# Where a decoder trunk computes the second layer's first eight modulation panels

## The reference

```python
mod = (silu(c) @ ada_w[l] + ada_b[l]).reshape(B, 9, D)      # 9 chunks of 1024: shift, scale, gate x 3
sh1, sc1, g1, sh2, sc2, g2, sh3, sc3, g3 = mod              # per sequence, broadcast over tokens
u = rmsnorm(x, ng[0]) * (1 + sc1) + sh1
x = x + 0.5 * g1 * swiglu(u, w_ffn_up[l, 0], w_ffn_down[l, 0])
u = rmsnorm(x, ng[1]) * (1 + sc2) + sh2
# in projection; conv, RWKV, pooling and attention branches; four gated branch products; out projection
merged = sum(sigmoid(u @ w_gate[l, i]) * (y_i @ w_branch[l, i]))
x = x + g2 * (merged @ w_out[l])
u = rmsnorm(x, ng[2]) * (1 + sc3) + sh3
x = x + 0.5 * g3 * swiglu(u, w_ffn_up[l, 1], w_ffn_down[l, 1])
```

## Time and profile before

| | |
|---|---|
| median of three runs | 3191.99 us |
| the profiled execution, its own time | 3193.19 us |
| its span (first to last instruction) | 3191.5 us |
| TensorE matmuls busy | 3124.6 us, 98% |
| VectorE, GpSimd, ScalarE busy | 1170.4, 858.4, 421.1 us |
| granted TensorE clock, mean | 0.993 |

### The profile page before, as it was taken

The page is one execution under the profiler, slowest core; times in us unless marked ns, Lnnn a source line. Parts: engine busy times, 40 slices in busy tenths (PEclk is TensorE's granted clock), DMA queues, the critical chain, the costliest instruction groups (busy, mean ns, idle before and its releaser), DMA issues.

```text
span 3191.5 us, 42629 instructions
## 1 busy us (share of the span) xinstructions
PE 3124.6 (98%) x17664; PEld 2478.5 (78%) x17664; DVE 1170.4 (37%) x2229; ACT 421.1 (13%) x806; POOL 858.4 (27%) x749
## 2 busy tenths in 40 slices
PE   7999999999999999999989999999999999999998
PEld 4777887677777878888867778876777778788887
DVE  3223422453233463343232233234533244633432
ACT  2000002302111120010010000023021111200100
POOL 2333430210000334444333334302100003344442
PEclk9999999999999999999999999999999999999999
DMA  6444322531111212222254442234311113122221
GB/s 268 182 161 185 112 86 93 172 124 39 51 51 58 103 66 80 80 90 75 87 225 160 170 178 106 86 107 146 126 53 51 37 60 111 67 79 81 88 73 65
DMA packets 72928, 337.43 MB, mean 106 GB/s; under 512 B 10528, under 2 KB 27680, under 8 KB 39584
## 3 DMA queue, kind: packets, MB, share of 16 engines
q1 hardware_dynamic: 63360, 312.03, 27.0%
q0 software_dynamic: 6816, 18.88, 2.0%
q10 hardware_dynamic: 2560, 3.80, 0.3%
HBM read 326.55 MB, written 6.02 MB: 104 GB/s over the span
## 4 chain that ended last, share of the span: by engine, by line
PE 96%; DVE 2%; DMA 1%; ACT 1%; issue 0%; SPq 0%; DVEq 0%
PE ps L670 95%; DVE ws L1683 1%; ACT ws L1404 0%; DMA ring<-w_ada 0%; DMA lp<-params 0%; DVE u L1683 0%; DVE proj L1683 0%; ACT u L1404 0%; PE ps L725 0%; DVE masked_room L2054 0%; DVE x L1686 0%; PE ps L1231 0%; DVE masked_room L1683 0%; DVE proj L1686 0%; DVE proj L1689 0%
## 5 line engine op out<-in xcount | busy, mean ns | idle before, releaser
L670 PE MATMUL ps<-u,ring 128*128 128x272 f32 x4608 | 1152.3, 400 | 23.4 <-ACT u L1404 17.4
L670 PEld LDWEIGHTS ps<-u,ring 128*128 128x128 f32 x4608 | 865.6, 192 | 238.8 <-issue 50.9
L1683 DVE TENSOR_TENSOR ws<-ws,ps 128x272 f32<-128x272 f32 (+2 forms) x778 | 347.3, 452 | 1484.6 <-PE ps L670 1477.9
L633 POOL TENSOR_TENSOR masked_room<-ring 128x512 f32<-128x512 f32 (+1 forms) x76 | 95.8, 1261 | 1312.2 <-DVE pause L2380 657.0
L670 PE MATMUL ps<-y,ring 128*128 128x272 f32 x1376 | 350.8, 393 | 0.0
L1404 ACT ACTIVATE ws<-ps 128x272 f32<-128x272 f32 (+1 forms) x398 | 154.9, 396 | 1322.0 <-PE ps L670 1321.7
L670 PE MATMUL ps<-y,masked_room 128*128 128x272 f32 x1296 | 315.8, 393 | 2.8 <-DVE ws L1683 2.8
L670 PE MATMUL ps<-y,ws 128*128 128x272 f32 x1296 | 315.6, 393 | 0.0
L670 PEld LDWEIGHTS ps<-y,ring 128*128 128x128 f32 x1376 | 261.3, 190 | 54.5 <-DVE proj L1683 0.7
L670 PEld LDWEIGHTS ps<-y,masked_room 128*128 128x128 f32 x1296 | 245.7, 190 | 55.4 <-issue 4.8
L670 PEld LDWEIGHTS ps<-y,ws 128*128 128x128 f32 x1296 | 245.9, 190 | 52.0 <-issue 1.6
(11 more groups left out here) (199 smaller groups left out, 2516.7 us busy)
## 6 DMA issues: line engine op xcount, KB each, us to landing
ring<-w_up SPq DMA_DIRECT2D x88, 1024.0 KB, 4.8
ring<-w_ada SPq DMA_DIRECT2D x72, 1024.0 KB, 4.8
ring<-w_down SPq DMA_DIRECT2D x32, 1024.0 KB, 4.7
ring<-w_gate SPq DMA_DIRECT2D x32, 1024.0 KB, 4.7
ring<-w_in SPq DMA_DIRECT2D x22, 1024.0 KB, 4.7
ws<-cache SPq DMA_DIRECT2D x128, 128.0 KB, 3.1
ws<-cache POOLq DMA_DIRECT2D x128, 128.0 KB, 3.4
ring<-w_down SPq DMA_DIRECT2D x16, 768.0 KB, 4.1
```

The costliest lines, as they stand in the source:

```text
L633: nc.gpsimd.tensor_tensor(sums[:, 0], a21, a22, ALU.add).then_inc(w_sums.sem, 1)
L670: return nc.tensor.matmul(out, lhsT, rhs, start=start, stop=stop, skip_group_check=skip)
L1683: return V.tensor_tensor(out, a, b, op)
```

## The change

Five edits:

1. The first 8 modulation panels of the second layer are computed in the first layer's up1, behind units 2, 4, ..., 16 (`NEXT_AT`), and their two chunks are turned and kept there. The second layer has no stage ada: it starts with `sum_squares`. The small part of `lp` (the layer's vectors) for it is loaded in up1. All numbers of loads and parts now run on over both layers.
2. `keep_clock` issues matmuls of constants (128 x 260) whose results nobody reads: 4 before each up0 and up1, 3 more inside unit 0 of the first up0, 3 before each in, 2 in the sample attention of each layer.
3. The gate of fill 5 goes into bank 6, and waits for the sigmoid of fill 3 only.
4. The final store of `x` is five DMAs: three of two tiles each, as they are done, then tile 7, then tile 6.
5. The large loads of constants and layer parameters stand before load 12 of up0, not before load 3.

```diff
+NEXT_AT = [[q // 2 - 1] if q in range(2, 18, 2) else [] for q in range(FT)]
+def panels_behind(l, f, q):
+    if f == 0:
+        return ADA_AT[q]
+    return NEXT_AT[q] if l + 1 < DEPTH else []
...
+        def gate_bank(f):
+            return 6 if f == 5 else 4
...
-                        if stage == "up0" and i == 3:
+                        if stage == "up1" and i == 3 and l + 1 < DEPTH:
+                            sp_.wait_ge(mix_done.sem, mix_done.upto(l, 1))
+                            sp_.dma_start(lp[:, 0:NVEC], lp_d[l + 1][:, 0:NVEC]).then_inc(lp_loaded.sem, 16)
+                        if stage == "up0" and i == 12:
                             if l == 0:
                                 sp_.dma_start(cst[:, MASKS:NCST], cst_d[:, MASKS:NCST]).then_inc(mask_loaded.sem, 16)
                             sp_.dma_start(lp[:, NVEC:NLP], lp_d[l][:, NVEC:NLP]).then_inc(lp_rest_loaded.sem, 16)
...
-            sp_.wait_ge(x_done.sem, x_done.upto(DEPTH, 0))
-            sp_.dma_start(o_y, x[:, :, :]).then_inc(y_stored.sem, 16)
-            sp_.wait_ge(y_stored.sem, 16)
+            for p in range(3):
+                sp_.wait_ge(x_done.sem, x_done.upto(DEPTH - 1, 16 + 2 * p + 2))
+                sp_.dma_start(o_y[:, 2 * p:2 * p + 2, :], x[:, 2 * p:2 * p + 2, :]).then_inc(y_stored.sem, 16)
+            for done, tile in ((23, 7), (24, 6)):
+                sp_.wait_ge(x_done.sem, x_done.upto(DEPTH - 1, done))
+                sp_.dma_start(o_y[:, tile, :], x[:, tile, :]).then_inc(y_stored.sem, 16)
+            sp_.wait_ge(y_stored.sem, 5 * 16)
...
+            def keep_clock(n, bank):
+                for _ in range(n):
+                    mm(ps[:, bank, 0:MASKS], cmat(ONES), cst[:, 0:MASKS])
...
             def ffn(l, f):
                 if f:
                     sum_squares(l, 2)
+                    keep_clock(4, 5)
+                elif l:
+                    sum_squares(l, 0)
+                    keep_clock(4, 5)
                 else:
                     for n in range(ADA_FIRST):
...
+                    keep_clock(4, 5)
...
                         product(bx, w(0, 0), tok(0, 0), True, u0=0)
-                        s1 = panel(l, f"up{f}", up_place(f, 1))
+                        if l == f == 0:
+                            keep_clock(3, 5)
+                        s1 = panel(l, f"up{f}", up_place(l, f, 1))
...
-                    if f == 0:
-                        for i in ADA_AT[q]:
-                            modulation(l, panel(l, "up0", ADA_PLACE[i]), ADA_FIRST + i)
+                    for n in panels_behind(l, f, q):
+                        modulation(l + f, panel(l, f"up{f}", UP_ORDER[l][f].index(("ada", n))), n)
...
-                            pe_.wait_ge(fill_gate.sem, fill_gate.upto(l, f))
+                            pe_.wait_ge(fill_gate.sem, fill_gate.upto(l, f - (f == 5)))
...
                 if n == 0:
-                    copy_modulation(l, CHUNK - 1)
-                    copy_modulation(l, 2 * CHUNK - 1)
+                    if l == 0:
+                        copy_modulation(l, CHUNK - 1)
+                        copy_modulation(l, 2 * CHUNK - 1)
...
-                    if n == 0 and q - 1 in CHUNK_DONE:
-                        keep_modulation(l, CHUNK_DONE[q - 1])
+                    if chunk_done(l, n, q - 1) is not None:
+                        if n:
+                            dve.wait_ge(lp_loaded.sem, lp_loaded.upto(l + 1, 1))
+                        keep_modulation(l + n, chunk_done(l, n, q - 1))
+                        if n and chunk_done(l, n, q - 1) == 1:
+                            modulation_factors(l + 1, 2, (0,), ())
```

More of the change, by code:

```diff
@@ L144, with up_order, chunk_done @@
 for _i in range(ADA_UP):
[L145 to L150, removed]
+    ADA_AT[3 * (_i // CHUNK) + (min(_i % CHUNK, 2) if _i < 6 * CHUNK else _i % CHUNK)].append(ADA_FIRST + _i)
+NEXT_AT = [[q // 2 - 1] if q in range(2, 18, 2) else [] for q in range(FT)]
[3 more added lines that the diff above has]
+    return NEXT_AT[q] if l + 1 < DEPTH else []
+def up_order(l, f):
+    return [e for q in range(FT) for e in [("up", q)] + [("ada", n) for n in panels_behind(l, f, q)]]
+UP_ORDER = [[up_order(l, f) for f in range(2)] for l in range(DEPTH)]
+def chunk_done(l, f, q):
+    last = [n for n in panels_behind(l, f, q) if n % CHUNK == CHUNK - 1] if q >= 0 else []
+    return last[0] // CHUNK if last else None
 DOWN_CHUNKS = ((0, 4), (4, 4), (8, 3))
@@ L158 @@
 SEVEN_CHUNKS = (DOWN_CHUNKS, ((0, 4),), DOWN_CHUNKS)
-STAGES = [("ada", ADA_FIRST, ADA_FIRST), ("up0", FT + ADA_UP, FT + ADA_UP),
-          ("down0", DOWN, DOWN), ("in", 11, 44), ("gate", 24, 2 * FILLS), ("gate_b", 8, 8),
-          ("out", 4, 4), ("up1", FT, FT), ("down1", DOWN, DOWN)]
+STAGES = [([] if l else [("ada", ADA_FIRST, ADA_FIRST)]) +
+          [("up0", len(UP_ORDER[l][0]), len(UP_ORDER[l][0])), ("down0", DOWN, DOWN), ("in", 11, 44),
+           ("gate", 24, 2 * FILLS), ("gate_b", 8, 8), ("out", 4, 4),
+           ("up1", len(UP_ORDER[l][1]), len(UP_ORDER[l][1])), ("down1", DOWN, DOWN)] for l in range(DEPTH)]
 UNIT0, UNITS = {}, 0
@@ L165 @@
     UNITS += _k
[L166 to L174, removed]
+LOAD0, PART0 = [{} for _ in range(DEPTH)], [{} for _ in range(DEPTH)]
+LOADS = PARTS = 0
+for _l in range(DEPTH):
+    for _n, _k, _m in STAGES[_l]:
+        LOAD0[_l][_n], PART0[_l][_n] = LOADS, PARTS
+        LOADS, PARTS = LOADS + _k, PARTS + _m
 TURNS_AT = {("in", 4): (0,), ("in", 8): (1, 2), ("in", 9): (3,), ("in", 10): (4,), ("gate", 0): (5,),
@@ L181, in load_number, with up_place, ada_part @@
 def load_number(l, stage, i):
-    return l * LOADS + LOAD0[stage] + i
-def up_place(f, q):
-    return UP_PLACE[q] if f == 0 else q
+    return LOAD0[l][stage] + i
+def up_place(l, f, q):
+    return UP_ORDER[l][f].index(("up", q))
+def ada_part(l, n):
+    if n >= ADA_FIRST:
+        return PART0[l]["up0"] + UP_ORDER[l][0].index(("ada", n)) + 1
+    if l:
+        return PART0[l - 1]["up1"] + UP_ORDER[l - 1][1].index(("ada", n)) + 1
+    return PART0[l]["ada"] + n + 1
 def unit_of(stage, i):
@@ L199, in in_half, with last_part @@
     return (j, c, hf) if j else (j, hf, c)
-def last_part(stage, n):
+def last_part(l, stage, n):
     if stage == "ada":
@@ L211, in last_part @@
         k = n + 1
-    return PART0[stage] + k
+    return PART0[l][stage] + k
 VEC_LINKS, ACT_LINKS, RW_LINKS = 145, 15, 5
@@ L544, in source @@
                     return w_ada[l * 36 + i]
[L545 to L548, removed]
+                if stage in ("up0", "up1"):
+                    f = int(stage[-1])
+                    kind, n = UP_ORDER[l][f][i]
+                    return w_up[l * (2 * FT) + f * FT + n] if kind == "up" else w_ada[(l + f) * 36 + n]
                 if stage.startswith("down"):
@@ L556, in source @@
                     return (w_branch if i % 2 else w_gate)[l * 16 + (first + i // 2)]
-                f, n = int(stage[-1] == "1"), {"u": FT, "o": 4}[stage[0]]
-                per = (2 if stage[:-1] == "up" else 1) * n
-                return srcs[stage][l * per + (i + f * n)]
+                return w_out[l * 4 + i]
             def cache_loads(l, turn):
@@ L573, in _ @@
                 sp_.wait_ge(wkv_stored.sem, wkv_stored.upto(l, 0))
-                for stage, n, _ in STAGES:
+                for stage, n, _ in STAGES[l]:
                     for i in range(n):
@@ L750, in ffn @@
                 for q in range(FT):
-                    place, unit, sums_at = up_place(f, q), f * FT + q, 4 * unit_of(f"up{f}", q)
+                    place, unit, sums_at = up_place(l, f, q), f * FT + q, 4 * unit_of(f"up{f}", q)
                     s = load_number(l, f"up{f}", place) % R
@@ L783, in ffn @@
                     product(by, ws_(1), ts_(1), True)
-                    if f == 0 and q - 1 in CHUNK_DONE:
-                        turn_modulation(l, CHUNK_DONE[q - 1])
+                    if chunk_done(l, f, q - 1) is not None:
+                        turn_modulation(l + f, chunk_done(l, f, q - 1))
                     if q:
@@ L1013, in fill @@
                         k = j if gate else j - KT
-                        m = mm(ps[:, 4 if gate else 5, 0:HALF],
+                        m = mm(ps[:, gate_bank(f) if gate else 5, 0:HALF],
                                ring[:, slots[not gate], k * 256 + c * P:k * 256 + c * P + P],
@@ L1412, in copy_modulation @@
                 chunk = n // CHUNK
-                stage, k = ("ada", n + 1) if chunk < 2 else ("up0", ADA_PLACE[n - ADA_FIRST] + 1)
-                act.wait_ge(part.sem, part.upto(l, PART0[stage] + k))
+                act.wait_ge(part.sem, part.upto(0, ada_part(l, n)))
                 act.wait_ge(mod_pe.sem, mod_pe.upto(l, chunk))
```

40 lines of the change are left out of this document (20 added, 20 removed).

## The result

| | before | after |
|---|---|---|
| median of five runs of each | 3194.04 us | 3176.06 us |
| lowest and highest | 3190.69 to 3194.86 | 3174.78 to 3177.43 |
| profiled execution, its own time | 3193.19 us | 3176.12 us |
| its span | 3191.5 us | 3174.4 us |
| granted TensorE clock, mean | 0.993 | 0.998 |

The account below looks back on a forecast made before the run. TensorE was taken to bound the kernel, ending the chain for 96% of the span. Terms -14.3 + 10.0 - 5.2 - 4.2 - 2.0 - 1.0 + 0.5 = -16.2 us gave 3177.0, median forecast 3175.8 us, range 3171 to 3183.

Parts of the forecast that it names:

- Second layer's start: From the last large addition into x to up0's dense work: stage ada goes, -14.3 us (bounds -12.0 and -15.2).
- a held addition: Second layer's start: GpSimd's sums could hold a VectorE add up to 1.6 us; left out, as sums end before last adds.
- Panels in up1: First layer's up1: eight panels and two turns in a dense stretch cost +10.0 us (bounds +9.4 and +10.6).
- Rival 4: Up1 starves, TensorE waiting for every modulation panel's landing: 38.4 us more, +22 or 3214 us; chance 0.02.
- Fill 5: Both layers: with bank 6 the gate matmuls start 2.6 us earlier, -5.2 us in all (bounds -4.4 and -5.3).
- rival 2: At fill 5 something else holds the gate or branch part; 2.6 us return at fill 6: 3181.0 us, chance 0.09.
- Final store: End of the kernel: only tile 6 is issued last and lands in 2.4 us, -4.2 us (bounds -3.8 and -4.5).
- the sign named: End of the kernel: a last store landing in 2.1 to 2.8 us would show the forecast.
- Unread matmuls: They keep the clock up: -2.0 us before in, -1.0 before up1, +0.5 before first up0, 0 in sample attention.
- the +0.5: First up0: unread matmuls start late at low clock, partly recovered, +0.5 us (bounds -1.0 and +2.6).
- Rival 1: Unread matmuls do not hold the clock, or cost as much as they bring: -10.9 or 3181.1 us, chance 0.16.
- rival 3: All starts stay at 2.4 GHz: -18.6 or 3173.4 us, chance 0.10.

Follow-up runs that it names:

- e5_panels_only: The kernel before with only the move of the eight modulation panels into the first layer's up1: 3189.98 us, ratio 0.9992.
- e1_no_unread: The changed kernel with no unread matmul anywhere, all else kept: 3181.58 us, ratio 0.9964.
- e3_one_bank: The changed kernel with the gate of fill 5 back in bank 4 and its old wait: 3184.94 us, ratio 0.9972.
- e9_sums_early: The changed kernel without GpSimd's wait for the end of out before the weight sums of up1's unit 0: 3174.53 us, ratio 0.9943.
- e8_panels_in_waits: The changed kernel without first up0's unread matmuls; panels 0, 1 before first layer's up1 and 8, 9, 10 before second up0 replace unread ones: 3176.69 us.
- e11_four_ahead: e9_sums_early without first up0's unread matmuls; panels 0, 1 before first layer's up1 and 8, 9 before second up0 replace unread ones: 3168.91 us.
- e4_one_store: The changed kernel with a single final store of all of x again: 3180.18 us, ratio 0.9957.

## Why the prediction was right

The forecast was 0.3 us from the median, and that close by luck. The difference itself was forecast as 16.2 us; the two profiled executions differ by 17.07 and the medians by 18.0, since two more runs of the kernel before raised its median from the 3191.99 of the forecast to 3194.04. The terms, one by one:

- **Second layer's start**, predicted -14.3, measured -14.52. The move alone gave 13.48 of it in `e5_panels_only`; without unread matmuls the start took 17.09 us there and 16.28 in `e1_no_unread`, so they are worth 0.2 to 1.0 in these two profiles. Three parts of it can be read: no wait for `ring<-w_ada` in the chain; GpSimd's sums over at 1602.47, before the norm; and tiles of `u` at the pace of the earlier trace rows:

```profile
1611.89 5.17 DVE L1729 TENSOR_TENSOR u<-x,ws 128x544 f32<-128x544 f32 x8 [3.47 <-ACT ws L1450]
```

  The reason given for leaving out a held addition was only half right. The sums did reach the additions: one stood 0.99 us instead of 0.50. The term does not show it because the addition lies 4.7 us before the last but one, while TensorE was still busy with the last products. The two tiles of the earlier trace rows end 0.58 us behind GpSimd's sum (1172.39 - 1171.81), where the prediction puts one tile's 0.65.

```profile
1601.78 0.99 DVE L1732 SCALAR_TENSOR_TENSOR x<-ws,mod,x 128x272 f32<-128x272 f32 x1
```

```profile
1601.21 1.26 POOL L670 TENSOR_TENSOR masked_room<-ring,masked_room 128x512 f32<-128x512 f32 x1
```

- **Panels in up1**, predicted +10.0, measured +10.02. The rows that answer to the earlier trace rows, from TensorE's timeline, show one of the eight: 4.87 us from the start of the product before it to the start of the second behind it, two products taking 3.67, so 1.20 for the panel, and no wait in brackets.

```profile
1209.86 2.00 PE L702 MATMUL ps<-u,masked_room 128*128 128x272 f32 x8
1211.79 1.07 PE L702 MATMUL ps<-ring,csil 128*32 128x256 f32 x16
1212.79 2.10 PE L702 MATMUL ps<-u,ring 128*128 128x272 f32 x8
1214.73 2.00 PE L702 MATMUL ps<-y,ws 128*128 128x272 f32 x8
```

  Rival 4 (a stall for each panel) would have shown there.
- **Fill 5**, predicted -5.2, measured -5.47, a little outside the bounds of -4.4 and -5.3. Fill 6 starts at 762.90 without a wait, so rival 2 did not occur. `e3_one_bank` shows that the wait can be dearer than the profile of before says: 8.65 us where it also costs the clock.
- **Final store**, predicted -4.2, measured -4.56. The term was undersized, and a little outside its bounds of -3.8 and -4.5: 272 KB land in 2.0 us, faster than the 135 KB of another queue in the earlier trace rows (2.1), where the value taken was 2.4 and the sign named was 2.1 to 2.8. The estimate from the Trainium skill (DMA: Bandwidth & Descriptors, section Anatomy of one DMA), 2.6 us, is for another issue path and here too high; the measurement decides.
- **Unread matmuls**, predicted -2.5 in sum, measured -2.56 over the same five places in one profile. The sum agrees by luck, its parts do so only before in (-1.17 and -1.42, shown by `e1_no_unread`). Before up1 the 1.29 of one layer cannot be put down to them: without them `e1_no_unread` took 17.5 us in both layers, 0.2 to 0.3 more than after. In the first up0 the trace shows +1.32, of which 0.64 is there when the last panel lands (34.03 against 33.39), ahead of the first unread matmul; over all profiles it lands between 33.12 and 35.02. The 0.68 behind it lie within the spread of the profiles without unread matmuls, so the +0.5 is not shown. Rival 1 (the matmuls bring nothing) is refuted for in and holds for up1 and the first up0; rival 3 (clock up at all starts) is refuted, since it falls at both starts of up1.

What the prediction did not see: it took the length of up1's start for a matter of clock and of TensorE's waiting. The earlier trace rows had the cause of the 17.3 us, GpSimd's sum over the norm; the clock adds 1.3 only where it stays low for longer, as at 18.61. The prediction used this for the second layer's start and not for up1, where `e9_sums_early` found 1.3 us a start.

Errors of both signs helped: +0.8 us in the first up0 stands against -0.6 before in, -0.4 at the store, -0.3 at fill 5, -0.3 before up1 and -0.2 at the second layer's start.

## What to carry to other kernels

Work that only has to be moved pays by the difference of two places: what TensorE waits at the old one, less what the work costs in the new. In a dense stretch it costs all of its time (here 10.0 of 13.5 us); the place to look for is a wait of TensorE itself, and there it can stand in place of matmuls that are issued for the clock alone. Before an operation is moved ahead of a norm, look at what the order of loads then does to GpSimd: one up panel that lands 10 us later (`e8_panels_in_waits` against `e11_four_ahead`) cost the norm 3.3 us and the clock on top.

## What the runs showed of the hardware that was not expected

- Eight `tensor_tensor` operations of 128 x 544 on VectorE took 5.17, 6.50 or 8.45 us, with none of GpSimd's 128 x 512 sums beside them, with one and a part of another, and with three and a part. GpSimd's own sums went from 1.26 to 1.76 us. The Trainium skill (SBUF — State Buffer, section Who interferes with whom) has both engines excluding each other for a whole instruction, and the traces agree: the tile that VectorE began at 1609.03 beside a sum in `e8_panels_in_waits` took 1.79 us instead of 0.65, and ended 0.58 us behind that sum.
- The clock falls at some passes and not at others of the same stage: the start of up1 took 17.33 us in the first layer of `e4_one_store` and 18.69 in the second, the eight matmuls behind a 2.5 us wait 3.93 (before) or 5.43 us (`e3_one_bank`), the stretch of the sample products 173.5 or 175.1 us. Of such a place one profile shows a sample and no price. Nor does every fall cost time: up1 took 17.32 us with one (after) and without (`e8_panels_in_waits`).
- A store of 272 KB landed in 2.0 us, one of 2176 KB in 6.6, both from SyncE's queue.
- A modulation panel (eight matmuls with 32 columns of weights and 256 of data) has a record of 1.07 us and adds 1.20 to a dense stretch, the same in up1 as in up0, with its 1 MB load on the way. Two in a row have a record of 1.93 us.
